# Value projections after the conv projections, the sample softmax in two parts, and value pages read two groups an item

## What is computed

```
z = rms_norm(x) @ w_in                  # 3072 columns: u, gb, gc, q, k, v (and 8 forget columns)
a = gb * causal_dwconv(gc * u)          # three taps
att_prompt = softmax(q k^T / 8 + f_i - f_j, causal) @ v            # 1024 tokens
k_past, v_past = cache_k[page_table], cache_v[page_table]          # 8 sequences x 32 pages x 128 tokens
att_sample = softmax(q_s [k_past, k_s]^T / 8 + bias) @ [v_past, v_s]
x = x + concat(a, att) @ w_out
```

## Time and profile before

| | us |
|---|---|
| median of 3 runs | 2822.16 (2821.26 to 2825.33) |
| the profiled execution | 2822.6, its span 2820.0 |
| projections, 24 units | 83.2 to 350.1 |
| attention, first matmul to first of the output projection | 359.9 to 648.2 |
| all behind it | 648.2 to 2820.0 |

### The profile page before, as it was taken

One profiled execution on the slowest core, in us unless ns is written; L12 is line 12 of the kernel. 1 busy time (PEld: TensorE's weight loads), 2 busy tenths in 40 slices (PEclk: granted clock), 3 DMA queues, 4 the chain that ended last, 5 costly groups with the idle time before them and its releaser, 6 DMA issues.

```text
span 2820.0 us, 40852 instructions
## 1 busy us (share of the span) xinstructions
PE 2594.2 (92%) x16562; PEld 2462.8 (87%) x16562; DVE 1269.6 (45%) x1428; ACT 678.4 (24%) x961; POOL 886.8 (31%) x555
## 2 busy tenths in 40 slices
PE   6999948889899999999997898879899999999995
PEld 4999935459799999999996898879899999999995
DVE  5889974433643333333336300462543333333336
ACT  4321134442321111111113312231222111111112
POOL 3767620002243333333332211152243333333330
PEclk9999958999999999999998999988999999999998
DMA  3988647983011111111111211423111111111111
GB/s 137 316 316 272 236 169 264 351 296 113 31 53 45 45 51 45 45 45 45 45 51 30 97 43 61 110 105 109 30 46 48 49 45 45 45 50 46 45 40 60
DMA packets 121893, 287.08 MB, mean 102 GB/s; under 512 B 20245, under 2 KB 21142, under 8 KB 121274
## 3 DMA queue, kind: packets, MB, share of 16 engines
q1 hardware_dynamic: 84762, 170.86, 17.1%
q10 hardware_dynamic: 36736, 113.72, 13.0%
q0 software_dynamic: 288, 1.05, 0.1%
HBM read 263.38 MB, written 22.18 MB: 101 GB/s over the span
## 4 chain that ended last, share of the span: by engine, by line
PE 73%; DVE 13%; issue 4%; ACT 4%; DMA 3%; SPq 2%; POOL 1%; DVEq 0%; ACTq 0%; POOLq 0%
PE G L663 65%; DVE KTMP L1650 3%; DMA XT<-in_ck 2%; DVE XT L1636 2%; PE G L708 2%; DVE QT L1617 1%; SPq L546 1%; PE M L812 1%; DVE KT L1594 1%; PE G L881 1%; ACT XT L1340 1%; PE G L853 1%; PE M L899 1%; DVE XT L1737 1%; DMA HF<-in_cv 1%
## 5 line engine op out<-in xcount | busy, mean ns | idle before, releaser
L2063 POOL TENSOR_TENSOR WLO<-WRAW,WHI 128x1024 fp32r<-128x1024 f32 x192 | 466.0, 2433 | 1365.6 <-ACT WHI L1425 834.2
L663 PE MATMUL G<-HHI,WHI 128*128 128x344 f32 x3408 | 730.1, 323 | 10.6 <-ACT QT L1131 4.6
L663 PE MATMUL G<-HLO,WHI 128*128 128x344 f32 x3408 | 727.0, 322 | 0.0
L663 PE MATMUL G<-HHI,WLO 128*128 128x344 f32 x3408 | 723.1, 321 | 0.0
L663 PEld LDWEIGHTS G<-HHI,WHI 128*128 128x128 f32 x3408 | 577.2, 189 | 13.2 <-issue 9.7
L663 PEld LDWEIGHTS G<-HLO,WHI 128*128 128x128 f32 x3408 | 580.3, 190 | 0.0
L663 PEld LDWEIGHTS G<-HHI,WLO 128*128 128x128 f32 x3408 | 571.5, 189 | 0.0
L1850 DVE TENSOR_TENSOR XT<-XT,G 128x1032 f32<-128x1032 f32 x192 | 236.0, 1229 | 397.3 <-PE G L663 397.1
L663 PE MATMUL G<-HIDH,WHI 128*128 128x344 f32 x1056 | 227.0, 324 | 14.0 <-issue 14.0
L1425 ACT ACTIVATE WHI<-WRAW 128x1024 fp32r<-128x1024 f32 x108 | 112.3, 1056 | 494.0 <-PE G L663 494.0
L663 PE MATMUL G<-HIDL,WHI 128*128 128x344 f32 x1056 | 224.9, 321 | 0.0
(11 more groups left out here) (306 smaller groups left out, 2512.7 us busy)
## 6 DMA issues: line engine op xcount, KB each, us to landing
WRAW<-in_w ACTq DMA_DIRECT2D x192, 512.0 KB, 3.6
XT<-in_ck SPq DMA_DIRECT2D x244, 256.0 KB, 4.5
HF<-in_cv SPq DMA_DIRECT2D x152, 256.0 KB, 5.1
XT<-in_cv SPq DMA_DIRECT2D x104, 256.0 KB, 5.1
XT<-in_xp SPq DMA_DIRECT2D x2, 4096.0 KB, 16.8
x_scr<-XT SPq DMA_DIRECT2D x1, 4128.0 KB, 11.7
XT<-x_scr SPq DMA_DIRECT2D x1, 4128.0 KB, 12.2
out_y<-XT SPq DMA_DIRECT2D x8, 516.0 KB, 3.0
```

Of the source, the lines that this page charges most:

```text
L663: mm = pe.matmul(out[:, c], w, x[:, c * TC:(c + 1) * TC], start=first and n == 0, stop=last and n == 2)
L2063: TT(WLO[:, s], WRAW[:, s], WHI[:, s].bitcast(F32), ALU.subtract).then_inc(w_lo, 1)
```

## The change

- Unit order: the four conv triples come at places 8 to 19 (CONV), the value units at 20 to 23 (VALUE). unit_at maps a place to its weights. Value tile j is transposed after unit 21 + j, the last one after ScalarE's pair_high(0).
- K_PLAN: 56 groups in the projections (1 at place 0, 3 at each of places 1 to 7, then 3, 2, 1 over and over at the conv places and 3, 3, 3, 1 at the value places), eight late: the whole eighth sequence, one group an item in items 0 to 7. For these key_own (VectorE's two pages) stands between attend and normalise and takes the query row from QB in SBUF; key_rest (the sum of GpSimd's two pages of the group before) stands behind normalise.
- Softmax of sequences 0 to 6: maximum at the end of the projections, shift and Exp in item 0. Of the eighth: maximum in item 8, shift and Exp in item 9. The sum over all in item 10.
- Values: 2 groups an item from item 1 (VALUE_SPREAD), 3 or 2 from item 25, the last two in item 30. Three homes until all keys are summed (the first 16 groups), five after that. SyncE's loop runs over items: value groups whose home is free at that item, then one key group; the wider homes first in item 8, behind a wait for all key sums.

```diff
-K_PLAN = {u: (3 if u else 1) if u < 12 else (3, 2, 1)[(u - 12) % 3] for u in range(24)}
+CONV, VALUE = 8, 20
+K_PLAN = {u: (3, 2, 1)[(u - CONV) % 3] if CONV <= u < VALUE else 3 if u else 1 for u in range(23)}
+K_PLAN[23] = 1
 K_LATE = GROUPS - sum(K_PLAN.values())
 
 K_FIRST = GROUPS - K_LATE
-K_STEPS = -(-K_LATE // 2)
-EARLY = K_STEPS + 1
-V_FIRST = EARLY + 1
-V_STEPS = 24
-VALUES = []
-for _k in range(STEPS):
-    _had = VALUES[-1] if VALUES else 0
-    _due = max(0, -(-(_k - V_FIRST) * GROUPS // V_STEPS))
-    VALUES.append(min(_due, _had - _had % 8 + 8, GROUPS))
+assert K_LATE == 8
+LAST_MAX = K_LATE
+LAST_SHIFT = LAST_MAX + 1
+LAST_SUM = LAST_SHIFT + 1
+VALUE_SPREAD = [2, 2, 2, 2] * 6 + [3, 3, 2] * 2
+VALUES = [sum(VALUE_SPREAD[:_k]) for _k in range(STEPS)]
 BATCH_MASKED = {min(_k for _k in range(STEPS) if VALUES[_k] >= 8 * (_b + 1)): _b for _b in range(B)}
+V_NARROW = VALUES[K_LATE]
...
+def unit_at(u):
+
+    if CONV <= u < VALUE:
+        return u + NW
+    return u - VALUE + CONV if VALUE <= u < 24 else u
...
-    return (g % KSLOTS * KD * 512, KD * 512), (ND * T + 2 * T + g % 2 * (PG - KD) * 512, (PG - KD) * 512)
+    return (g % 2 * PG * 512, KD * 512), ((g % 2 * PG + KD) * 512, (PG - KD) * 512)
...
+def value_home(g):
+
+    return g % 3 if g < V_NARROW else (3, 4, 0, 1, 2)[(g - V_NARROW) % VSLOTS]
+
+
+def value_uses(g):
+
+    return sum(value_home(e) == value_home(g) for e in range(g))
+
+
+def value_loadable(g):
+
+    last = max((e + 1 for e in range(g) if value_home(e) == value_home(g)), default=0)
+    return max(min(k for k in range(-1, STEPS) if (VALUES[k] if k >= 0 else 0) >= last),
+               K_LATE if value_home(g) >= 3 else -1), last
...
-            for g in range(GROUPS):
+            for g in range(K_FIRST + 2):
...
-            for g in range(GROUPS):
+            def values_in(g):
                 pages = pages_of(g)
-                if g < 2:
-                    sp.wait_ge(tile_done, T_IE + 24)
-                elif g < 4:
-                    sp.wait_ge(kd_red, GROUPS - 2 * (3 - g))
-                elif g < 5:
+                wait(sp, v_used, value_loadable(g)[1])
+                for j in range(PG):
+                    page_in(a["cv"], pages[j], VSLOT[value_home(g)][:, j], v_loaded[value_home(g)])
+
+            sp.wait_ge(tile_done, T_IE + 24)
+            for k in range(-1, STEPS):
+                if k == K_LATE:
+                    sp.wait_ge(kd_red, GROUPS)
                     sp.wait_ge(kp_red, GROUPS)
-                else:
-                    sp.wait_ge(v_used, g - VSLOTS + 1)
-                for j in range(PG):
-                    page_in(a["cv"], pages[j], VSLOT[g % VSLOTS][:, j], v_loaded[g % VSLOTS])
-                if g == 4:
-
                     sp.wait_ge(k_added, B)
                     sp.dma_start(PW[:], a["pw"]).then_inc(par_in, 16)
+                for g in range(GROUPS):
+                    if value_loadable(g)[0] == k:
+                        values_in(g)
+                if 1 <= k and K_FIRST + 1 + k < GROUPS:
+                    keys_in(K_FIRST + 1 + k)
...
-                if 9 <= u <= 12:
-                    values_turned(u - 9, 0)
+                if u > VALUE:
+                    values_turned(u - VALUE - 1, 0)
+            values_turned(NW - 1, 0)
...
                     act.dma_start(o["k"][j], KT[:, j]).then_inc(act_outs, 16)
-                elif u < 12:
-                    if j == 0:
-                        act.wait_ge(kd_red, K_WIDE)
-                        act.wait_ge(kp_red, K_WIDE)
+                elif u >= VALUE:
                     if j >= 2:
-
                         act.wait_ge(tmp_out[j % 2], 16)
+                    elif j:
+                        act.wait_ge(a_saved, 16 * NW)
+                    else:
...
             pair_high(0)
+            values_turned(NW - 1, 0)
...
+            def batches_exp(b0, b1):
+                act.wait_ge(sshift, 2 if b0 else 1)
+                flat = SCR[:, b0:b1].rearrange("p b g h -> p (b g h)")
+                A(flat, flat, ACT.Exp).then_inc(sprob, 1)
...
+                if k == 0:
+                    batches_exp(0, B - 1)
...
+                if k == LAST_SHIFT:
+                    batches_exp(B - 1, B)
...
+                row = M1[:] if g < K_FIRST else QB[:, b % 2]
+                dve.wait_ge(kd_loaded[g % KSLOTS], 16 * KD * (g // KSLOTS + 1))
+                ring = key_pages(g)[0]
+                TT(ring, ring, row.rearrange("p (a f) -> p a f", a=1).to_broadcast([P, KD, NW * P]), ALU.mult
+                   ).then_inc(kd_mul, 1)
+                wait(dve, k_added, b - 1)
+                key_sums(g, ring, 0, kd_mul, kd_red)
+
+            def key_rest(g):
+
+                key_sums(g - 1, key_pages(g - 1)[1], KD, k_mul, kp_red)
+                if g % 8 == 0:
+                    b = g // 8
+                    dve.wait_ge(kp_red, g)
+                    dve.wait_ge(kd_red, g)
+                    TT(SCR[:, b - 1], SCR[:, b - 1], KTMP[:, (b - 1) % 2], ALU.add).then_inc(k_added, 1)
 
...
+            key_rest(K_FIRST)
+            dve.wait_ge(k_added, B - 1)
+            nc.vector.tensor_reduce(MX[:, 0:B - 1], SCR[:, 0:B - 1].rearrange("p b g h -> p b h g"), AX.X, ALU.max
+                                    ).then_inc(smax_ready, 1)
             pair_low(0)
...
             for k in range(STEPS):
                 attend(k)
+                if k == 0:
+                    batches_shift(0, B - 1)
+                if k < K_LATE:
+                    key_own(K_FIRST + k)
                 normalise(k)
-                for g in range(2 * k, min(2 * k + 2, K_LATE)):
-                    key_group(K_FIRST + g)
-                if k == K_STEPS:
-                    sample_max()
-                elif k == EARLY:
-                    sample_shift()
-                elif k == V_FIRST:
+                if 1 <= k <= K_LATE:
+                    key_rest(K_FIRST + k)
+                if k == LAST_MAX:
+                    batches_max(B - 1, B)
+                elif k == LAST_SHIFT:
+                    batches_shift(B - 1, B)
+                    TT(c4(0), QT[:, :, TP:T], KT[:, :, TP:T], ALU.mult).then_inc(qk_new, 1)
+                elif k == LAST_SUM:
                     sample_norm()
...
-            for g in range(GROUPS - K_LATE, GROUPS):
+            def batches_peak(b0, b1):
+                pool.wait_ge(smax_ready, 2 if b0 else 1)
+                nc.gpsimd.partition_all_reduce(MXA[:, b0:b1].rearrange("p b h -> p (b h)"),
+                                               MX[:, b0:b1].rearrange("p b h -> p (b h)"), P, RMAX
+                                               ).then_inc(smax_all, 1)
+
+            batches_peak(0, B - 1)
+            for g in range(K_FIRST, GROUPS):
                 key_products(g)
-
-
-            pool.wait_ge(smax_ready, 1)
-            nc.gpsimd.partition_all_reduce(MXA[:].rearrange("p b h -> p (b h)"), MX[:].rearrange("p b h -> p (b h)"),
-                                           P, RMAX).then_inc(smax_all, 1)
+            batches_peak(B - 1, B)
```

More of the change, by code:

```diff
@@ L328, in trunk @@
         QHI = [HLO[:, NW + j] for j in range(NW)]
-        VSLOT = [pages_at(x, at, PG) for x, at in ((HF[:, 1], 0), (HF[:, 1], PG * 512), (XF, 0), (XF, PG * 512),
-                                                   (HF[:, 0], 2 * T))]
+        VSLOT = [pages_at(x, at, PG) for x, at in ((HF[:, 1], 0), (HF[:, 1], PG * 512), (HF[:, 0], 2 * T), (XF, 0),
+                                                   (XF, PG * 512))]
         XSQ = SM[:, 0:2].rearrange("p k (c b) -> p (k c) b", b=B)
@@ L1272, in _ @@
                     A(FHI[:, 0:TP], GB[:, 0:TP], ACT.Copy).then_inc(att_in_hi, 1)
-                if u >= 12 and (u - 12) % 3 == 0:
-                    if u == 12:
+                if CONV <= u < VALUE and (u - CONV) % 3 == 0:
+                    if u == CONV:
                         act.wait_ge(gw_lo, 1)
-                        act.wait_ge(tmp_out[1], 32)
-                        act.wait_ge(vt_psum, 2 * NW)
                     else:
@@ L1351, in _ @@
                     pair_high(k // NB + 1)
-                if k == EARLY:
-                    act.wait_ge(sshift, 1)
-                    flat = SCR[:].rearrange("p b g h -> p (b g h)")
-                    A(flat, flat, ACT.Exp).then_inc(sprob, 1)
+                if k == LAST_SHIFT:
+                    batches_exp(B - 1, B)
             turned(STEPS - 1)
@@ L1694, in _ @@
                 for _ in range(K_PLAN.get(u, 0)):
-                    key_group(key[0])
+                    key_own(key[0])
+                    if key[0]:
+                        key_rest(key[0])
                     key[0] += 1
-                if u >= 12 and kind == 1:
+                if kind == 1:
                     if jc == 0:
-                        dve.wait_ge(tmp_out[1], 32)
-                        dve.wait_ge(vt_psum, 2 * NW)
                         dve.wait_ge(pool_const, 2)
@@ L1715, in _ @@
```

(28 more changed lines are left out.)

63 lines of the change are left out of this document (26 added, 37 removed).

## The result

The change makes the kernel slower: 2829.0 us, median of 13 runs (2825.68 to 2832.14), beside 2823.55 for the kernel before on the same chip (13 runs, 2819.23 to 2829.67). The ratio is 1.0016, with a 95% interval of 1.0009 to 1.0024: about 4.5 us, and inside the 0.2% that the prediction took as its bound for a change. The forecast of 2806 us, and its range to 2820, missed it.

The account below looks back on a forecast made before the run. TensorE sets the projections' pace, VectorE holds the first eight attention items, and TensorE and DMA are near their limits in later quick ones. Gains 6.3 + 3.3 + 2.2 + 1.8 + 2.2 + 0.5 = 16.3 from 2822.2 give 2806 us, range 2789 to 2820.

Parts of the forecast that it names:

- a new stall of 4.1 us: Projections, unit 11: TensorE waits 4.1 us for a bank until VectorE's first conv multiplication; VectorE then catches up.
- That makes about 9 us an item, 62 us for seven: Items 1 to 7: late key pages pace about 9 us an item, 62 us instead of 70.6, gain 10.5.
- A: Stretch from the first bias matmul to that of item 8 (items 0 to 7): predicted 80.4 us, before 88.1.
- The term of 1 us an item for normalisation beside the product: Items 1 to 7: 1 us an item added because VectorE's normalisation slows next to GpSimd's product.
- TensorE stands about 6 us: Items 8 and 9: TensorE idles about 6 us for value groups 16 and 17, leaving 6.3 of 10.5 gained.
- B: Stretch from the first bias matmul of item 8 to the scores of item 10: predicted 27.0 us, before 22.8.
- Items 10 to 31: Later attention items: two value groups an item instead of 2.67, gains of 3.3, 1.8, about 2.2 per pair start, 0.5.
- C: Stretch from the scores of item 10 to the output projection: predicted 167.5 us, before 177.5.
- (a): Early items: busy TensorE at 2.4 GHz, quick landings, 7.6 us an item, smaller item 9 bubble; about 2793; chance 0.25.
- (b): Little or no change: conv stall grows or repeats, groups 16 and 17 cost 12 us; 2816 to 2820; chance 0.13.
- (c): Items 1 to 7: key wait takes over, GpSimd's product holding key_own and normalise; 2840, half of it 2823; chance 0.10.
- The clock: First attention items: expected to begin at 1.2 GHz again, after TensorE's idle stretch of 8.5 us.

Follow-up runs that it names:

- Old order: Changed kernel with the projections' unit order of the kernel before, still 56 key groups there: 2822.3 us, 0.9984 of the kernel before.
- Keys ahead: Changed kernel with VectorE's two late key pages issued before the item's value groups: 2820.1 us, 0.9989 of the kernel before.
- narrow 18: Changed kernel with value groups 16 and 17 in the three early homes, loaded ahead of the wait for key sums: 2816.3 us, 0.9975 of the kernel before.
- Own behind: Changed kernel with key_own of the eight late groups after normalise instead of ahead of it: 2825.9 us, 1.0010 of the kernel before.
- product behind: Changed kernel with GpSimd's product of each late key group held until normalise is done: 2824.1 us, 1.0000 of the kernel before.
- three-edits kernel with the old order: Changed kernel with Keys ahead, narrow 18, product behind and Old order joined: 2796.8 us, 0.9898 of the kernel before.

## Why the prediction was wrong

**The projections: nearly right, in part by luck.** "a new stall of 4.1 us" at unit 11: measured 3.02 at 194.78, and 1.07 at 230.18, where the prediction has VectorE catching up and no stall. Together they are 4.1 in this trace; in the five other traces of the new order the same two stalls sum to 3.2 to 5.9. Unit 23 ended at 349.9 (predicted 348.6), and the tail of 8.5 us took 8.6. But the gain was credited to the new order. Old order shows that the order costs and the 56 groups gain.

**Item 0: right.** Turns(0) began 18.3 us after the first bias matmul, predicted 18.1.

**Items 1 to 7: the first step that failed**, "That makes about 9 us an item, 62 us for seven". They took 70.9. The pace is set once in two items, by the chain from one big item to the next. From t, the end of item 3's value groups (405.77), the key's pages landed at t + 9.7 (the prediction took 9.5); multiplication and sum took 2.7 (2.4); from there it was 1.6 to the transposes (0.9, and 1 for the product); transposes and item 5's two value groups took 6.4, until 426.12. That is 20.4 us, and the chains before and behind it, until 405.77 and until 446.52, are 20.4 too, with landings at t + 9.7 and t + 10.0.

Of the prediction's 18 us for two items its other terms leave 4.2 for transposes and value groups, which is near its prices for 2.4 GHz; the granted clock from 399.30 to 405.77, from 419.75 to 426.12 and from 440.28 to 446.52, each time right behind a wait of 5.5 to 6.5 us, was 0.55 to 0.56. With the prices that the same paragraph has for the lower clock (3.6 and 3.45) two items would have come to 20.9. So the mechanism was right, and the sum took the cheap end of "17 to 20": by these figures, as an estimate, the clock is some 2.2 of the 2.4 us missed in each of three chains. Another 1.6 stands in item 0's transposes, where TensorE waits for the second half of a normalisation that GpSimd held to 3.80 us. Together that is most of the 8.6 missed.

Keys ahead shows the other side: without the late pages the same items ran at 0.96, and A fell by 12. The landing alone was close, but also partly by luck: issue until t + 5.5 and the median of 4.9 from the earlier trace rows give t + 10.4, not 9.5, and in the small items, where it cost nothing, the pages landed at t + 11.5 to 11.7. The term of 1 us an item for normalisation beside the product measured 0.9 in the mean of items 2 to 7 (2.18, 2.21, 2.10, 0.75, 1.94 and 1.79 against 1.28, 0.62, 1.15, 0.75, 1.02 and 0.88).

**Items 8 and 9: the second**, "TensorE stands about 6 us". It stood 6.0 and 0.8, as the mechanism said. The term left out what the work behind the idle stretch costs: it ran at a granted clock of 0.52 and took 4.1 us more than the same work in narrow 18. Of the 5.8 missed in B the rest, about 1 us, was not followed.

**Items 10 to 31: too large for this trace.** C gained 6.5 instead of 10.0. Items 10 to 15 took 40.7 (predicted 39.7) and 18 to 23 37.6 (38.8), but the pair starts 24.0 (predicted 21.3, before 23.5) and 24.8 (predicted 23.6, before 25.8). That is not what a group less is worth, though. Own behind has the same code from item 10 on, and its pair starts took 21.3 and 22.6, its C 166.5. The clock differs: 0.92 there and 0.79 in after in the first of them, and the same two value groups (first two rows after, last two own behind) take

```profile
524.24 1.80 PE L837 MATMUL M<-HF,SCR 128*32 128x512 f32 x8
525.79 1.95 PE L837 MATMUL M<-XT,SCR 128*32 128x512 f32 x8
...
523.59 1.06 PE L837 MATMUL M<-HF,SCR 128*32 128x512 f32 x8
524.48 1.04 PE L837 MATMUL M<-XT,SCR 128*32 128x512 f32 x8
```

What makes the clock rise in one profile and not in the other stays open.

**The rivals.** (a) and its quick landing did not come. (b) was nearer than the forecast: one of its two reasons came. It had groups 16 and 17 cost 12 us instead of 6, and wait and slower work in item 9 cost 10.9. The conv stall did repeat, but in this trace the sum stayed at 4.1. (c) named the right place, and the result lies beside its half price of 2823; its mechanism was not the one, though. Keeping GpSimd's product away was worth 4.5 us of time, by product behind, where (c) wanted 17 or more, and none of the eight multiplications by QB was held; the late pages were the larger part. And an item took 10.1 us, less than the 11.4 from which (c) was to decide: item 9 and C made up the difference.

**The clock** behaved as forecast at the start (0.50 from 358.5 to 376.8). That it would matter behind every wait of items 2 to 6, and in item 9, was missed.

## What to carry to other kernels

When one queue issues loads for two consumers, order them by who is late; then look at the waits inside a group of issues, since a wait for one home holds all loads behind it. Price an idle stretch of TensorE as the wait and the slower work behind it, and take the price of that work from rows at the clock that such stretches show. When a change takes several steps at once, run the cheap ones alone: here two key groups less gave what the reordering was credited with. And before a few us between two profiles are put down to an edit, look how far the same code spreads in the others.

## What the runs showed of the hardware

- VectorE is held to the end of a GpSimd product that began before it. In the three-edits kernel with the old order the product ran from 374.74 to 377.10, and the multiplication by QB that began at 375.17 ended at 378.17, 1.07 after it, for 3.00 us instead of 1.22. Keys ahead has the same with other times: a product from 431.12 to 433.49, a multiplication from 432.36 to 434.56, again 1.07 behind it. The pair of tensor_scalar was caught in five of items 2 to 7 of the kernel after. The Trainium skill (SBUF — State Buffer, Who interferes with whom) says that the port pair shared by the two engines is an exclusive lock, that a VectorE instruction with two SBUF inputs contends with a GpSimd one that reads SBUF, and that tensor_scalar can contend when it runs in a two-port mode; these rows agree for both forms.
- An idle stretch of 6.0 us in item 9, behind transposes at a granted clock of 0.50, was followed by 9.7 us at 0.52. In narrow 18 the transposes ran at 0.50 too, and without the wait the 4.7 us behind them ran at 1.00.
- The same code got different clocks: from the biases of item 16 to the scores of item 18 it took 24.0 us at 0.79 in the kernel after and 21.3 us at 0.92 in own behind.
- Behind the output projection, where the kernels have the same code, single profiles took 2171.8 to 2178.1 us. And C took 166.5 us in own behind and 171.8 in old order, whose code is the same from item 10 on. A difference of 6 us between two spans is therefore not yet one of the edit; no run here shows what makes it.
